# Both prompt attentions rewritten to walk the queries row by row, with normalised, turned and split weights

## The reference, cut to what matters

```python
def block(xs):                       # one block of 128 queries
    s = jnp.einsum('bqhd,bkhd->bhqk', qi, k) * scale
    if per_frame: mask = k_pos[None, :] <= pi[:, None]                       # FoX
    else:         mask = k_chunk[None, :] <= (pi // CHUNK)[:, None]          # MLA, chunks of 64
    if decay:     s = s + (li - lk_t)                                        # FoX: cumulative log-forget sums
    s = jnp.where(mask[None, None], s, -jnp.inf)
    p = jax.nn.softmax(s, axis=-1)
    return jnp.einsum('bhqk,bkhd->bqhd', p, v)
...
o = jnp.concatenate([o_mla, o_fox], axis=-1) @ w_out
```

## Time and profile before

| | us |
|---|---|
| median of 3 runs | 2565.74 |
| range | 2563.72 to 2568.56 |
| span of the profiled execution | 2561.9 |
| its PE busy | 2406.9 (94%) |
| its DVE, ACT, POOL busy | 1462.4 (57%), 922.2 (36%), 791.7 (31%) |

### The profile page before, as it was taken

How to read it: one execution, slowest core, us unless ns; L and a number is a source line. 1 busy time by engine, 2 the same in 40 slices (tenths; PEclk the granted TensorE clock), 3 DMA queues, 4 the chain that set the end, 5 groups by cost and what they waited for, 6 DMA issues and landing times. The chain is left out here.

```text
span 2561.9 us, 43347 instructions
## 1 busy us (share of the span) xinstructions
PE 2406.9 (94%) x15501; PEld 2162.4 (84%) x15501; DVE 1462.4 (57%) x2356; ACT 922.2 (36%) x1779; POOL 791.7 (31%) x701
## 2 busy tenths in 40 slices
PE   4999999999989999899989899996999999999985
PEld 4999999998867789778866688785999999998864
DVE  7766666655587323345533455446866666655576
ACT  6322222233454112444433355434322222233443
POOL 1544443434462000011011122023444344434452
PEclk8999999999999999899999999997999999999998
DMA  4344444367665221010054400123344444456663
GB/s 152 120 146 137 159 142 142 130 202 238 189 216 181 106 70 44 25 30 0 1 201 166 149 1 0 50 83 99 101 159 142 142 148 133 145 181 222 194 211 140
DMA packets 244152, 326.40 MB, mean 127 GB/s; under 512 B 31825, under 2 KB 138449, under 8 KB 242001
## 3 DMA queue, kind: packets, MB, share of 16 engines
q1 hardware_dynamic: 244048, 325.06, 38.5%
HBM read 230.31 MB, written 94.69 MB: 127 GB/s over the span
## 5 line engine op out<-in xcount | busy, mean ns | idle before, releaser
L62 PE MATMUL ffn_bank<-x_hi,ffn_w_w_hi 128*128 128x256 f32 (+1 forms) x2464 | 736.7, 299 | 24.3 <-DVE x_lo L969 24.3
L63 PE MATMUL ffn_bank<-x_lo,ffn_w_w_hi 128*128 128x256 f32 (+1 forms) x2464 | 734.5, 298 | 0.0
L64 PE MATMUL ffn_bank<-x_hi,ffn_w_w_lo 128*128 128x256 f32 (+1 forms) x2464 | 734.3, 298 | 0.0
L62 PEld LDWEIGHTS ffn_bank<-x_hi,ffn_w_w_hi 128*128 128x128 f32 x2464 | 472.5, 192 | 26.7 <-DVE x_lo L969 26.7
L63 PEld LDWEIGHTS ffn_bank<-x_lo,ffn_w_w_hi 128*128 128x128 f32 x2464 | 473.0, 192 | 0.0
L64 PEld LDWEIGHTS ffn_bank<-x_hi,ffn_w_w_lo 128*128 128x128 f32 x2464 | 472.8, 192 | 0.0
L738 POOL TENSOR_TENSOR ffn_split_dn_lo<-ffn_in_dn_raw,ffn_split_dn_hi 128x512 fp32r<-128x512 f32 x176 | 251.0, 1432 | 285.1 <-ACT ffn_split_dn_hi L805 281.1
L724 POOL TENSOR_TENSOR ffn_w_w_lo<-gu_raw,ffn_w_w_hi 128x512 fp32r<-128x512 f32 x176 | 239.6, 1363 | 300.9 <-ACT ffn_w_w_hi L755 300.9
L1001 DVE TENSOR_TENSOR ffn_split_a_lo<-ffn_in_a_raw,ffn_split_a_hi 128x512 fp32r<-128x512 f32 (+2 forms) x176 | 220.7, 1271 | 170.7 <-ACT ffn_split_a_hi L807 170.6
L62 PE MATMUL ffn_bank<-ffn_split_dn_hi,ffn_split_a_hi 128*128 128x512 f32 x704 | 278.2, 395 | 18.9 <-DVE ffn_split_a_lo L1001 15.8
L724 POOL TENSOR_TENSOR ffn_w_w_lo<-ffn_w_s,ffn_w_w_hi 128x512 fp32r<-128x512 f32 x132 | 193.7, 1469 | 299.3 <-ACT ffn_w_w_hi L755 299.3
(11 more groups left out here) (401 smaller groups left out, 3948.1 us busy)
## 6 DMA issues: line engine op xcount, KB each, us to landing
gu_raw<-in_w_ffn_gu SPq DMA_DIRECT2D x88, 512.0 KB, 5.2
ffn_w_w_raw<-in_w_ffn_down SPq DMA_DIRECT2D x22, 1024.0 KB, 5.0
a_rows<-ffn_w_a_st SPq DMA_DIRECT2D x44, 512.0 KB, 2.9
t_rows<-ffn_w_w_raw SPq DMA_DIRECT2D x88, 256.0 KB, 2.4
s_rows<-ffn_w_a_st SPq DMA_DIRECT2D x88, 256.0 KB, 2.3
ffn_in_dn_raw<-in_w_ffn_down SPq DMA_DIRECT2D x88, 256.0 KB, 3.7
ffn_in_dn_raw<-t_rows SPq DMA_DIRECT2D x88, 256.0 KB, 3.4
ffn_in_a_raw<-s_rows SPq DMA_DIRECT2D x88, 256.0 KB, 3.2
```

The costliest lines, as they stand in the source:

```text
L62: pe.matmul(out, w_hi, x_hi, start=first, stop=False)
L63: pe.matmul(out, w_hi, x_lo, start=False, stop=False)
L64: return pe.matmul(out, w_lo, x_hi, start=False, stop=last)
```

## The change

The attention is written twice, as `mla_prompt` and `fox_prompt`, and no longer loops in hardware: all 64 rows (head n, query tile t) are written out. A row g goes through these steps: PE scores its 128 queries against all (t+1)*128 keys; DVE takes the exact maximum from the scores in PSUM; ACT takes the exponential with the maximum as bias and the sum as a second output; DVE inverts the sum; POOL multiplies the row by it, in place; PE turns the row in 128x128 blocks (L1857 in FoX); ACT copies them to a hi part and DVE to a lo part, in groups of up to four blocks; PE multiplies values (now stationary, 64 columns, split into hi and lo) by up to 512 queries in three passes, which gives the output transposed, and ACT copies it into `acc` already turned. Scores run two rows ahead (LEAD). The rough scores, the turned maxima, the ones column and all dummy matmuls are gone. MLA's rotary keys are turned once for all heads; FoX's decay terms are turned once and brought to their rows by two small DMAs a head. The output projection turns only the sample tile on PE. SP loads two parts of `w_out` at the start of FoX and six once head 7 is prepared. In the diff, `mla_prompt` is given with its loops; those of `fox_prompt` have the same order on PE, ACT and DVE.

```diff
--- before.py
+++ after.py
@@ -1429,336 +1429,308 @@
+GROUPS = [(t, k0, min(k0 + HT, t + 1)) for t in range(PT) for k0 in range(0, t + 1, HT)]
...
+PREP_STEP = {1: 0, 2: 1, 3: 2, 4: 3}
+PV_LATE = {0: (0, 1), 1: (2, 3), 2: (4, 5), 3: (6, 7)}
+PV_EARLY = {6: (0, 1), 7: (2, 3)}
+V_STEP, LATE_OUT_STEP, EARLY_OUT_STEP = 3, 4, 0
+NP_ROWS = 3
+LEAD = 2
...
+def mla_prompt(nc, ident, ident_bf, mask_bf, q_rows, kv_rows, krope, acc, early_hi, early_lo, load_next, limit):
...
+    scale = QW ** -0.5
...
+        p = k.sb("p", [P, NP_ROWS, SEQ])
+        late_hi, late_lo = [k.sb(f"late_{n}", [P, PT, HALF], F32R) for n in ("hi", "lo")]
+        v_hi, v_lo = [[k.sb(f"v_{n}{b}", [P, PT, VD], F32R) for b in range(2)] for n in ("hi", "lo")]
...
+        scores = k.ps("scores", [P, 2, SEQ])
+        flip = k.ps("flip", [P, 2, HALF])
+        turn = k.ps("turn", [P, HALF])
+        out = k.ps("out", [P, HALF])
...
+                def score(g):
+                    n, t = divmod(g, PT)
+                    b, cols = n % 2, (t + 1) * P
+                    if t in (0, HT):
+                        pe.wait_ge(lo_ok, PREP * n + 2 * (t // HT) + 2)
+                        if n == 0:
+                            pe.wait_ge(key_lo, t // HT + 1)
+                        if n == 1 and t == 0:
+                            pe.wait_ge(key_copied, 2)
+                    if g >= LEAD:
+                        pe.wait_ge(exped, g - LEAD + 1)
+                    for c0 in range(0, cols, HALF):
+                        w = min(HALF, cols - c0)
+                        at = slice(c0, c0 + w)
+                        diagonal = c0 + w == cols
+                        last = split_product(pe, scores[:, g % 2, at], qT_hi[b][0:QW, t * P:t * P + P], qT_lo[b][0:QW, t * P:t * P + P],
+                                             kT_hi[b][0:QW, at], kT_lo[b][0:QW, at], True, not diagonal)
+                    last = pe.matmul(scores[:, g % 2, cols - P:cols], ident_bf[:, :], mask_bf, start=False, stop=True)
+                    last.then_inc(scored, 1)
+                def flip_row(g):
+                    pe.wait_ge(normed, g + 1)
+                    for x, k0, k1 in groups_of(g):
+                        if x >= 2:
+                            pe.wait_ge(pt_lo, x - 1)
+                        for c in range(k0, k1):
+                            last = pe.transpose(flip[:, x % 2, (c - k0) * P:(c - k0) * P + P], p[:, g % NP_ROWS, c * P:c * P + P], ident[:, :])
+                        last.then_inc(flipped, 1)
+                def values(n, h, pieces):
+                    b = n % 2
+                    for c in pieces:
+                        if c == 0:
+                            pe.wait_ge(pt_lo, groups_through(PT * n + HT * h + HT - 1))
+                            pe.wait_ge(v_lo_ok, n + 1)
+                            if h:
+                                if n:
+                                    pe.wait_ge(o_taken, 2 * n)
+                            elif n + 1 < H:
+                                pe.wait_ge(lo_ok, PREP * (n + 2))
+                        c0 = max(0, c - HT * h) * P
+                        dst = out_of[h][:, c0:HALF]
+                        high, low = pT_hi[h][:, c, c0:HALF], pT_lo[h][:, c, c0:HALF]
+                        pe.matmul(dst, v_hi[b][:, c, :], high, start=(c == 0), stop=False)
+                        pe.matmul(dst, v_hi[b][:, c, :], low, start=False, stop=False)
+                        last = pe.matmul(dst, v_lo[b][:, c, :], high, start=False, stop=(c == HT * (h + 1) - 1))
+                        if c == HT * (h + 1) - 1:
+                            last.then_inc(pv_ok, 1)
...
+                for g in range(-LEAD, ROWS):
+                    n, t = divmod(g, PT)
+                    if g + LEAD < ROWS:
+                        score(g + LEAD)
+                    if g >= 0:
+                        flip_row(g)
+                        if n + 1 < H and t in PREP_STEP:
+                            prep(n + 1, PREP_STEP[t])
+                        if n and t in PV_LATE:
+                            values(n - 1, 1, PV_LATE[t])
+                        if t in PV_EARLY:
+                            values(n, 0, PV_EARLY[t])
+                values(H - 1, 1, range(PT))
...
+                def exponent(g):
+                    n, t = divmod(g, PT)
+                    cols = (t + 1) * P
+                    act.wait_ge(maxed, g + 1)
+                    if g >= NP_ROWS:
+                        act.wait_ge(flipped, groups_through(g - NP_ROWS))
+                    act.activation(p[:, g % NP_ROWS, 0:cols], scores[:, g % 2, 0:cols], ACT.Exp, bias=nmax[:, g:g + 1], accum_out=total[:, g:g + 1]).then_inc(exped, 1)
+                def weights_high(g):
+                    hi, _, cols = weights(g)
+                    n, t = divmod(g, PT)
+                    for x, k0, k1 in groups_of(g):
+                        if n and t % HT == 0:
+                            act.wait_ge(pv_ok, 2 * (n - 1) + t // HT + 1)
+                        act.wait_ge(flipped, x + 1)
+                        act.activation(hi[:, k0:k1, cols], flip[:, x % 2, 0:(k1 - k0) * P].rearrange("p (k n) -> p k n", n=P), ACT.Copy).then_inc(pt_hi, 1)
...
+                for g in range(-LEAD, ROWS):
+                    n, t = divmod(g, PT)
+                    if g >= 0:
+                        weights_high(g)
+                    if g + LEAD < ROWS:
+                        exponent(g + LEAD)
+                    if g >= 0:
+                        if n + 1 < H and t in PREP_STEP:
+                            high(n + 1, PREP_STEP[t])
+                        if t == V_STEP:
+                            v_high(n)
+                        if n and t == EARLY_OUT_STEP:
+                            take(n - 1, 0)
+                        if n and t == LATE_OUT_STEP:
+                            take(n - 1, 1)
+                for h in range(HALVES):
+                    take(H - 1, h)
...
+                def maximum(g):
+                    n, t = divmod(g, PT)
+                    dve.wait_ge(scored, g + 1)
+                    dve.tensor_reduce(nmax[:, g:g + 1], scores[:, g % 2, 0:(t + 1) * P], axis=AX.X, op=ALU.max, negate=True).then_inc(maxed, 1)
+                def weights_low(g):
+                    hi, lo, cols = weights(g)
+                    for x, k0, k1 in groups_of(g):
+                        dve.wait_ge(pt_hi, x + 1)
+                        dve.tensor_tensor(lo[:, k0:k1, cols], flip[:, x % 2, 0:(k1 - k0) * P].rearrange("p (k n) -> p k n", n=P), plain(hi[:, k0:k1, cols]), ALU.subtract).then_inc(pt_lo, 1)
+                def invert(g):
+                    dve.wait_ge(exped, g + 1)
+                    dve.reciprocal(inverse[:, g:g + 1], total[:, g:g + 1]).then_inc(inverted, 1)
...
+                for g in range(-LEAD, ROWS):
+                    n, t = divmod(g, PT)
+                    if g + LEAD < ROWS:
+                        maximum(g + LEAD)
+                    if g >= 0:
+                        weights_low(g)
+                        if n + 1 < H and t in PREP_STEP:
+                            low(n + 1, PREP_STEP[t])
+                    if g + LEAD < ROWS:
+                        invert(g + LEAD)
...
+                def normalise(g):
+                    n, t = divmod(g, PT)
+                    row = p[:, g % NP_ROWS, 0:(t + 1) * P]
+                    pool.wait_ge(inverted, g + 1)
+                    pool.tensor_scalar(row, row, inverse[:, g:g + 1], None, ALU.mult).then_inc(normed, 1)
+                def v_low(n):
+                    pool.wait_ge(v_hi_ok, n + 1)
+                    pool.tensor_tensor(v_lo[n % 2][:, :, :], v_rows(n), plain(v_hi[n % 2][:, :, :]), ALU.subtract).then_inc(v_lo_ok, 1)
...
+def fox_prompt(nc, ident, ident_bf, mask_bf, decay, rows, loaded, acc, v_parts, decayT, load_first, load_rest):
...
+                def decay_rows(n):
+                    b = n % 2
+                    if n >= 2:
+                        sp.wait_ge(scored, PT * (n - 1))
+                    sp.dma_start(plain(q_tail[b][64:66, :]), plain(decayT[2 * n:2 * n + 2, :])).then_inc(decay_in[b], 16)
+                    sp.dma_start(plain(k_tail[b][66:68, :]), plain(decayT[2 * H + 2 * n:2 * H + 2 * n + 2, :])).then_inc(decay_in[b], 16)
+                sp.wait_ge(ones_ok, 4)
+                sp.wait_ge(decay_taken, 2)
+                decay_rows(0)
+                decay_rows(1)
+                load_first(sp)
+                for n in range(2, H):
+                    decay_rows(n)
+                sp.wait_ge(turned, PREP * H)
+                load_rest(sp)
...
+                        pe.matmul(scores[:, g % 2, at], q_both[b][:, tile], k_twice[b][:, at], start=True, stop=False)
+                        pe.matmul(scores[:, g % 2, at], q_tail[b][0:TAIL, tile], k_tail[b][0:TAIL, at], start=False, stop=not diagonal)
...
+                for g in range(-LEAD, ROWS):
+                    n, t = divmod(g, PT)
```

(22 more changed lines are left out.)

685 lines of the change are left out of this document (359 added, 326 removed).

## The result

The changed kernel takes 2621.86 us (median of 4 runs, 2620.44 to 2622.78) against 2565.91 (4 runs, 2563.72 to 2568.56): ratio 1.0222, 95% interval [1.0207, 1.0236]. The direction was forecast, the size was not: 2573.5 was expected, up to 2597 allowed for. The profiled span is 2619.5 us, 57.6 more than before. A run is some 2 us longer than its own span (2621.3 for 2619.5, before 2563.7 for 2561.9); the 4 us given above come from the profiled run of the kernel before having been the fastest of its runs.

What follows compares the result with a forecast made beforehand. PE's issue bounds the kernel before; in the changed one a chain of DVE, ACT and PE does. Span 2561.9 - 10.6 (stages) + 18.4 (clock falls) = 2569.7, plus 3.8 to the median: 2573.5 us; range 2545 to 2597, likeliest 2563 to 2582.

Steps and rivals of the forecast that it cites:

- POOL's price: POOL's multiplication of a weight row, in both attentions: taken as a copy's, 1.05 us for 1024 columns.
- the clock: PE in both attentions: falls to half clock after stands, 1.75 us each, in 9 of 10 FoX and 6 of 10 MLA heads: +18.4 us.
- the sum: Whole kernel: span 2561.9 - 10.6 from the stages + 18.4 from clock falls = 2569.7, median 2573.5 us.
- case (a): Whole kernel: the clock holds at the forecast's other prices, so 2555 us; chance 20%.
- The new chain: Attention heads: DVE and ACT take turns, then PE works in order; 21.2 us a head in MLA, 22.5 in FoX.
- Rival (c): POOL's multiplication costs two-input time: +0.5 to 1.5 us a head in MLA, +1.0 to 1.9 in FoX; 2584 to 2600; 15%.
- rival (d): Both attentions: more clock falls, or handovers of 0.1 instead of 0.03 us on the chain; 2585 to 2600 us; 10%.
- DVE's low part of row 5: MLA, step 6: PE waits for it before turning row 6, a stand of about 2.3 us per head.
- PE's serial part: PE's ordered work from its late wait to the next head's row 3: 6.4 us in MLA, 5.4 in FoX.
- V's low part: FoX, step 6: early value passes wait for POOL's `v_lo`, 1.2 us, made only behind the normalising of row 7.
- Row 2 of MLA's first head: Start of MLA: doubled chains and one table load bring this row to DVE at about 1118.
- the output projection: Stage after FoX: 64 transposes fewer save 6.2 to 7.0 us, an earlier first product 1: -7.5 us.

Runs made afterwards that it cites:

- the copies: Changed kernel with POOL's multiplication of each weight row made a plain copy of the row onto itself, in both attentions: 2593.21 us, 28.6 less than the changed kernel.
- the second run: Changed kernel without any pass of POOL over the weight rows, their division left out: 2568.07 us, 53.8 less than the changed kernel.

## Why the prediction was wrong

**The miss in three parts.** The measured 2621.9 lie 48.4 above 2573.5. The runs divide it: POOL's price, 28.6 (the copies); the clock, 22.1 by the run with copies and a PE kept at work, where the sum had 18.4, so 3.7; the chain, 2571.1 where case (a) had 2555, so 16.1. Together 48.4. That they add up so is no more than arithmetic; that the causes are independent is what the pairs of runs show (28.6 and 28.1, 22.7 and 22.1).

**The step that failed** is in "The new chain": "It reads one row and writes one, like the copy, so I take 1.05." The bounds were 1.05 and 2.1 to 2.9, and 2.84 lies in them. The choice was by likeness of operands, though no row showed an arithmetic operation of POOL at a copy's price: the only arithmetic rows, at 512 columns, were the dear ones. By the row of the same kind of work the other end was at least as near. Rival (c) had the mechanism and the sizes per head (up to 1.5 in MLA and 1.9 in FoX; the copies showed 1.3 and 1.9), and got 15%. It left out that the last head of each attention grows too: MLA's, from its row 3 to its last value product, took 25.4 us against 21.5 with the copies, FoX's 26.4 against 24.5.

**The range** went to 2597, about the upper end of (c) alone (2573.5 + 7 * 3.4); more falls and a longer chain stood only in rival (d), as another case with its own 2585 to 2600. The causes don't exclude each other, and here all three came together; their sum, 2573.5 + 28 + 16 + 4, was outside. Each was in the text with a price. The range was built from them as alternatives.

**The chain.** Its structure held: in MLA PE waits in step 6 for DVE's low part of row 5 once POOL is out of the way (2.16 us without its passes; 2.3 forecast), in FoX for `v_lo`; rows 3 to 7 took 12.8 and 12.4 us for 12.5 and 12.0. The mis-sized term is PE's serial part, 7.4 and 6.3 us for 6.4 and 5.4: in MLA four transposes put ahead of a wait that they stand behind, and in both no wait for DVE's low part of row 7. The sum has slips of its own: the terms written down for MLA give 6.9, and 6.4 only without score 0', which indeed stands in front of the wait; and the value passes of 256 and 128 columns, taken at 0.5, are 0.7 by the prices given (0.62 measured). By stages most of the 16.1 us lie in FoX, some 13, nine of them in its heads, each 1.3 too short in the sum. MLA is only some 3 us off, and that by luck: its heads are 1 us too short each, but its row 2 came at 1113.3 where 1117.2 was summed, and 3 us of this the stage had already when it began.

**The clock.** Without POOL's passes one fall costs 1.55 us in FoX and 1.6 in MLA (1.75 forecast); keeping the clock up is worth 22.7 us in the changed kernel and 22.1 with the copies (18.4 forecast). Of the 22.1, 9.5 lie in the MLA heads and 12.2 in those of FoX, where 7.4 and 11.0 were forecast: in MLA it falls in each head but the first and not in 6 of 10. How long it stays low says little by itself, as the seventh FoX head showed. The FoX heads of the second run show that the same stand of 2.4 us may or may not cost it, as the forecast had it.

**V's low part.** That the value products wait for it was forecast; that the order of two instructions on POOL is worth 3.2 us a head, more than the wrong price of the multiplication (1.9), was not looked at, since I priced the kernel as it stood.

**The other stages.** Row 2 of MLA's first head came to DVE at 1114.25 (1118 forecast), FoX's 9.7 us behind the stage's first transpose (8.7 forecast). From the output projection's first product to its last 104.4 us in place of 109.0, and its first comes 5.9 us behind the last value product, 7.8 before: 6.4 saved, 7.5 forecast. The late loads of `w_out` cost nothing, as forecast: the first product waited for DVE's split.

## What to carry to other kernels

Price an operation that the trace doesn't show by the row of the same engine and the same kind of arithmetic, not by how many tensors it reads; where the two ends of a price straddle the point from which it decides, its bad end belongs into the forecast's own range, added to the other errors and not set against them. When an engine's price falls out, ask what stood in its shadow: here a chain of DVE, ACT and PE (16 us) and the clock (22 us) beside POOL's 28. A wait at a fixed place in a serial engine is best filled with work that is due anyway (in MLA the value products one step sooner took away the falls and 1.3 us a head), and an instruction that many wait for goes ahead of long ones that few wait for.
